# Copying two projections out of PSUM in two halves each

## What is computed

```python
qkv_dn, z_dn, beta_logit, a_logit, qkv_mb, z_mb, merge_logit = jnp.split(h @ w_in, cuts, axis=-1)

qkv_dn = jax.nn.silu(causal_depthwise_conv(qkv_dn, conv_w))
q_dn, k_dn, v_dn = (to_heads(t_, DN_HEADS) for t_ in jnp.split(qkv_dn, 3, axis=-1))
...
o_dn = gated_delta_rule_chunked(l2_normalize(q_dn), l2_normalize(k_dn), v_dn, g, beta)
...
q_mb, k_mb, v_mb = (jnp.pad(to_heads(t_, MB_HEADS), ((0, 0), (0, 0), (0, pad), (0, 0)))
                    for t_ in jnp.split(qkv_mb, 3, axis=-1))
o_mb = moba_attention(q_mb, k_mb, v_mb)[:, :, :s]
```

## Time and profile before

| | us |
|---|---|
| median of 3 runs | 895.93 (895.84 to 895.93) |
| the profiled execution, its own time | 896.24 |
| its span, from the first to the last instruction | 894.4 |
| PE busy | 885.5 (99%) |
| DVE busy | 652.3 (73%) |
| ACT busy | 498.1 (56%) |
| POOL busy | 31.2 (3%) |

### The profile page before, as it was taken

The page is one execution under the profiler, slowest core; times in us unless marked ns, Lnnn a source line. Parts: engine busy times, 40 slices in busy tenths (PEclk is TensorE's granted clock), DMA queues, the critical chain, the costliest instruction groups (busy, mean ns, idle before and its releaser), DMA issues.

```text
span 894.4 us, 13339 instructions
## 1 busy us (share of the span) xinstructions
PE 885.5 (99%) x5610; PEld 757.1 (85%) x5610; DVE 652.3 (73%) x790; ACT 498.1 (56%) x676; POOL 31.2 (3%) x25
## 2 busy tenths in 40 slices
PE   9999999999999999999999999999999999999997
PEld 7889888888888888888888888888779998888885
DVE  6999656569777767699567977777668895556655
ACT  6865556465444454766566544445558784366624
POOL 0000000000000000000000000000000083000000
PEclk9999999999999999999999999999999999999999
DMA  9735443466666664544346666666336344324331
GB/s 360 271 143 175 156 141 141 141 244 222 240 228 240 228 243 166 202 156 166 117 144 253 229 242 228 241 236 235 142 127 243 126 142 143 114 100 157 136 133 47
DMA packets 24155, 165.40 MB, mean 185 GB/s; under 512 B 2688, under 2 KB 2944, under 8 KB 4896
## 3 DMA queue, kind: packets, MB, share of 16 engines
q1 hardware_dynamic: 22608, 159.73, 48.9%
q0 software_dynamic: 1056, 4.34, 1.3%
q10 hardware_dynamic: 432, 0.49, 0.2%
HBM read 163.50 MB, written 1.05 MB: 184 GB/s over the span
## 4 chain that ended last, share of the span: by engine, by line
PE 90%; DVE 6%; ACT 2%; DMA 1%; issue 1%; DVEq 0%; SPq 0%; ACTq 0%
PE acc L633 29%; PE lin L594 11%; PE lin L615 6%; PE lin L622 6%; PE lin L599 6%; PE lin L616 6%; PE lin L573 3%; PE lin L581 3%; PE lin L574 3%; DVE w_lo L1887 3%; PE acc L841 1%; PE acc L725 1%; PE acc L726 1%; DVE arena L2337 1%; PE acc L735 1%; PE lin L678 1%
## 5 line engine op out<-in xcount | busy, mean ns | idle before, releaser
L1887 DVE TENSOR_TENSOR w_lo<-raw,w_hi 128x2048 fp32r<-128x2048 f32 x137 | 318.3, 2337 | 126.1 <-ACT w_hi L1384 125.4
L1384 ACT CAST w_hi<-raw 128x2048 fp32r<-128x2048 f32 x137 | 259.3, 1907 | 135.8 <-DMA raw<-in_weights 90.8
L633 PE MATMUL acc<-w_hi,f_hi 128*128 128x512 f32 x288 | 113.1, 393 | 0.0
L633 PE MATMUL acc<-w_hi,f_lo 128*128 128x512 f32 x288 | 112.4, 390 | 0.0
L615 PE MATMUL lin<-w_hi,h_both 128*128 128x512 f32 x272 | 109.4, 402 | 0.2
L594 PE MATMUL lin<-h_both,w_hi 128*128 128x512 f32 x448 | 106.7, 390 | 0.0
L616 PE MATMUL lin<-w_hi,h_both 128*128 128x512 f32 x272 | 106.3, 391 | 0.0
L594 PEld LDWEIGHTS lin<-h_both,w_hi 128*128 128x128 f32 x448 | 83.2, 188 | 16.7
L633 PE MATMUL acc<-w_lo,f_hi 128*128 128x512 f32 x288 | 79.1, 389 | 0.3 <-DVE w_lo L1887 0.3
L622 PE MATMUL lin<-w_lo,h_both 128*128 128x512 f32 x272 | 68.2, 390 | 0.2 <-DVE w_lo L1887 0.2
L573 PE MATMUL lin<-h_both,w_hi 128*128 128x256 f32 x272 | 67.3, 287 | 0.0
(11 more groups left out here) (372 smaller groups left out, 1227.2 us busy)
## 6 DMA issues: line engine op xcount, KB each, us to landing
raw<-in_weights SPq DMA_DIRECT2D x149, 1024.0 KB, 4.8
rowbuf<-in_rows POOLq DMA_DIRECT2D x6, 512.0 KB, 3.9
x<-in_x_in SPq DMA_DIRECT2D x2, 512.0 KB, 4.4
raw<-in_weights SPq DMA_DIRECT2D x2, 512.0 KB, 7.1
arena<-in_const_even POOLq DMA_DIRECT2D x1, 1024.0 KB, 11.5
out<-x SPq DMA_DIRECT2D x3, 256.0 KB, 2.0
cst<-in_const SPq DMA_DIRECT2D x1, 580.0 KB, 10.2
out<-x ACTq DMA_DIRECT2D x1, 256.0 KB, 2.1
```

The costliest lines, as they stand in the source:

```text
L633: return pe.matmul(acc[:, at:at + 512], part_of(2 * j + k)[i][:, t * P:(t + 1) * P], w[:, k * 1024 + c * 512:k * 1024 + (c + 1) * 512], st ...
L1384: act.copy(w_hi[:, o % SPLIT, :], raw[:, j % RAW, :]).then_inc(hi_done, 1)
L1887: dve.tensor_tensor(w_lo[:, j % RAW, :], r, hi.bitcast(F32), ALU.subtract).then_inc(tile_split, 1)
```

## The change

The copy of `dv` and that of `bk` are each made by two instructions, one for each half of the PSUM pair. The first waits for the first tile alone (the first step of `tile_used`) and frees nothing; the second waits for the second tile and counts up `freed(name)`. For `dv` the first half is put between the exponential L1756 and the Silu of `q`, the second half where the whole copy stood. For `bk` the wait for `qg_ready` and the first half are put ahead of the cast that `split_until(LAST["bq"] + 4)` makes, the second half behind it. Both halves use the copy instruction in place of an activation with the function Copy. `copy_out` itself is not changed and goes on serving the other projections.

```diff
+            def half_out(name, i, dst):
+
+                act.wait_ge(tile_used, ORDINAL[FIRST[name] + i] + 1)
+                ins = act.copy(dst[:, i * 512:(i + 1) * 512], pair(name)[:, i * 512:(i + 1) * 512])
+                if i == 1:
+                    ins.then_inc(freed(name), 1)
...
             act.activation(srow(4), srow(2), ACT.Exp).then_inc(erow_ready, 1)
+            half_out("dv", 0, at("pre", 1024, 2048))
             conv_silu(S_AT["q"])
...
             load_exp()
-            copy_out("dv", at("pre", 1024, 2048), splits=False)
+            half_out("dv", 1, at("pre", 1024, 2048))
             split_until(LAST["dv"] + 1)
...
                 if l == 2:
+                    act.wait_ge(qg_ready, 1)
+                    half_out("bk", 0, at("bk"))
                     split_until(LAST["bq"] + 4)
-                    act.wait_ge(qg_ready, 1)
-                    copy_out("bk", at("bk"), splits=False)
+                    half_out("bk", 1, at("bk"))
```

## The result

The changed kernel takes 898.09 us (median of 8 executions, 897.16 to 898.89) beside 895.88 for the kernel before, measured with it: a ratio of 1.0024, with a 95% interval of 1.0015 to 1.0033. The eight executions fall into two groups, four at 897.16 to 897.56 with a mean granted clock of 0.998 to 0.999, and four at 898.62 to 898.89 with 0.996 to 0.997. No execution lies at the median itself, which is the middle of the gap between the groups. The profiled execution is one of the first group.

What follows compares the result with a forecast made beforehand. TensorE, busy 885.5 of 894.4 us, was taken as the bound; only the `bk` stall was added, 895.93+1.44 = 897.4 us, the `dv` gain counting only through DVE's 0.42. The range was 896.4 to 898.2 us, held at 84%.

Steps and rivals of the forecast that it cites:

- Part 1: At `dv`, copied in two halves: `dbeta` starts 0.40 us early, the Silus 0.70 late but covered, DVE's queue 0.42 ahead.
- Rival 4: At the first `dv` half, the table load isn't over when its row ends, taking 1.28 us more: 898.2 us; chance 4%.
- Part 2: At `bk`, the cast between the halves, behind the wait for `qg_ready`, delays `bv` from 739.17 to 740.61: +1.44 us.
- the third rival: In the stall before `bv`, PE's clock falls to 1.2 GHz for one fill: +5.7 us, about 903; chance 3%.
- Rival 1: Beside POOL, DVE's 0.42 us advance from `dv` doesn't reach `qg_ready`, which stays at 737.98: 897.8 us; chance 16%.
- rival 2: At `bk`, the new order costs nothing, `qg_ready` coming before ACT is free at about 735.5: 895.5 us; chance 10%.

Runs made afterwards that it cites:

- the second measurement: The changed kernel, unaltered, run once more beside the kernel before: median 897.43 us, ratio 1.0016 (11 executions).

## Why the prediction was right, and where it was not

**Part 1** held in each step. The first half stands at 697.07+0.31 = 697.38 (forecast 697.35), the table load right behind it, the Silus at 699.26 (699.26). PE's sums of squares were not late. `dbeta` starts at 707.11 (707.11), L1181 at 709.11: 0.20 ahead, not 0.27. The rule that was weighed, a drain of about 1.38 on top of each load (the Trainium skill, page "ScalarE: Activation LUTs", section "What ACT_TABLE_LOAD costs"), doesn't show: the copy ends and the load starts at 697.66, the load ends at 698.94, and the Silus start at 698.95. Rival 4 falls with it.

**Part 2** held too: first half at 737.57 (forecast 737.68), second at 739.85 (739.97), `bv` at 740.49 (740.61). The difference of 0.12 is nearly all one term: ACT's copy started 0.03 after `qg_ready`, not 0.12, for which an upper bound stood. So +1.32 for +1.44, and nothing was given back later: the stall and the span agree within the 0.1 to which spans are given. The lower group, four of eight executions at 897.16 to 897.56 and nine of eleven at 897.14 to 897.85, is what the sum of 897.4 described.

**The step that failed** is the third rival, PE's clock. I gave it 3%, because no stall of that length stood in the trace, and priced it as a whole fill at half clock, +5.7. It happened in 4 of 8 executions, then in 2 of 11, and cost 1.5, which is the size read in the run with `bk`'s halves alone. It should have been a term of the forecast with a chance near the middle, bounded above by 5.7 and below by nothing. It lifts the median from 897.3 to 898.09, over the bound of 0.2%: of my chances the 0.23 for slower came true, not the 0.74 for no change. That 898.09 still lies within the range, which ends at 898.2, is luck: with a fall in five executions of the eight instead of four the median would have been 898.6 or more. In the second measurement, with 2 of 11, the median is 897.43, 1.23 above the kernel before, and that is under the bound. What decides which executions pay is open. The prediction also took 0.1 us for the spread of the kernel before; eight executions spread over 0.74.

**Rival 1**, that DVE's advance doesn't arrive, did not happen. But its ground, the contention with POOL, was nearer to a decision than I thought. I took the length of DVE's stretch beside POOL as fixed. It has two values, 1.2 us apart at `qg_ready`, and the order of two starts decides between them; these lay 0.01 apart in the kernel before (DVE's split at 716.21, POOL at 716.20 in the earlier trace rows). With the other value the change would have cost next to nothing, which is most of the way to rival 2. The changed kernel came out on the bad side in both its traces, where POOL leads by 0.02 and 0.03, and by their times in all 19 executions; what gives POOL that lead was not tried.

## What to carry to other kernels

When a copy is split and other work put between its pieces, only the last piece frees the buffer: ask when the *first* piece may start, and add everything between to the time at which the buffer comes free. A wait that is harmless behind a long instruction need not be harmless ahead of it: here it also held up what PE needed and what stood behind that instruction, while with the cast last the same wait cost nothing. And price a new stall of TensorE at more than its length: after stalls of 1.7 us some executions here also paid for a clock that fell behind it, so look at all executions, not at the one that was profiled.

## What the runs showed of the hardware

- PE's clock fell to its lower level (products of 128x512 at 0.43 instead of 0.23) after stalls of 1.73 us in 6 of 19 executions, after stalls of 1.86 in 3 of 6, after 3.9 in 5 of 5, and in none of 10 where products filled the stall to 0.18. After a stall of 0.5 it fell in none of 11. In the kernel before with a stall added it fell in 3 of 6, and not in the profiled one, with its stall of 1.5. The stalls are those of one profiled execution each, and the counts go by time and mean clock; slow products were seen in two traces. After the stall of 1.86 the clock fell two products *after* PE had gone on, after that of 3.9 the first product was slow already. The fall cost about 1.5, and 1.4 to 3.0 after the longest stall.
- A DVE subtraction of 128x2048 that starts 0.01 to 0.04 after a POOL sum takes 4.5 (nine traces); one that starts at the same moment or 0.15 before takes 2.29 (one trace each). Such a tie is decided by hundredths of a microsecond and moved what came 20 us later by 1.2.
